# Weighing cached values eight pages at a time in every second tick of the first feed-forward stage

## The chip, the cores and the metric

The kernel runs on one core of a Trainium2 chip. The metric is the device time of one execution in microseconds (us), as the median of the runs. Fewer is better.

## The reference

One inference step of one layer, for a prompt of 1024 rows and for 8 samples of one row each, each with a past of 8192 positions in a paged cache (64 pages of 128 positions). The part that matters here, cut to its core:

```python
def half_ffn(x, g, w_gate, w_up, w_down):
    h = rmsnorm(x, g)
    return x + 0.5 * ((silu(h @ w_gate) * (h @ w_up)) @ w_down)
...
def sb_sample(q, k_new, v_new, bias, k_past, v_past):      # 8 samples, 8 heads of 64
    z = (q . [k_past, k_new]) * scale + bias
    w = sb_weights(z, q_pos, k_pos)       # exp(log_sigmoid(z) + sum of log_keep over later positions)
    o = w[..., :past] . v_past + w[..., past:] . v_new
...
x = half_ffn(x, ffn1 weights); then mixing (attention | state space), cross attention, half_ffn(ffn2 weights)
k_past = cache_k[l][page_table];  v_past = cache_v[l][page_table]
```

The product of the weights `w` with the cached values `v_past` is what the change moves. It adds up over all 64 pages of a sample.

## The kernel before, in words

The stages follow one another. The change is in `ffn1`, the first half feed-forward of the prompt (D_MODEL 1024, D_FF 2816), beside which the attention of the samples over the cache is done for six of the eight samples (scores for seven). The stage is a timetable of 132 ticks, written out by hand (`Timetable`), and every engine's program walks through the same ticks.

- **Feed-forward.** Twelve ticks make a group of 256 columns of D_FF. In ticks 0 to 7 of a group TensorE does one tile of 512 prompt rows of the gate or the up projection, in ticks 8 to 11 four tiles of the down projection. Each product of float32 quality is three matmuls (`three_passes`, L111 to L113) of split operands, so a tick has 24 such matmuls. VectorE and ScalarE split the weights (L84, L88), form the product of silu and up (L1763), and VectorE drains the down sums (`drain`, L1784). SP loads the weights.
- **Scores.** SP loads keys (`load_k`), 2 pages to a chunk in a ring of 4 chunks, and VectorE multiplies (L624) and reduces (L629) them: 32 chunks for a sample in 17 ticks (PERIOD).
- **Weights of a sample.** From its scores, ScalarE, VectorE and TensorE form the log weights: `page_sums` (L707) and `within_page` (L713) are single f32 matmuls that TensorE does at the end of a tick. L661 reads the result of L713.
- **Values.** GpSimd loads pages of values (`load_v`, L611) into a ring of VR = 8 pages, 256 KB each. TensorE weighs them in quads of four pages (`weigh`, L725): for each page c of four, a f32 matmul with 32 columns of weights and 512 columns of values, into rows 32c to 32c+31 of bank 6. In the trace each of these matmuls is two instructions, so a quad is eight. A sample has 16 quads. The last matmul of a quad adds one to `v_used`. Behind the last quad VectorE masks bank 6 (`own_heads`, L671), TensorE sums its columns (`columns`, L732) and ScalarE stores them.

The order on TensorE is `unit_tile` or four `down_tile` of the tick, and then `beside(t)`: first the quads of the tick, then `columns`, `page_sums` and `within_page`, each in its tick. Before a quad's matmul TensorE waits for the page (`v_in`). Before the load of page n GpSimd waits for the quad two quads earlier:

```python
def load_v(self, pool, n):
    if n >= self.VR:
        pool.wait_ge(self.v_used, n // 4 - self.VR // 4 + 1)
```

GpSimd's program loads the pages in their order and does nothing else in the stage after its constants. The quads of a tick are given by `Timetable.quads`: in the 17 ticks of a sample, ticks 0 to 13 have one quad each, tick 14 has two, ticks 15 and 16 none. Where a tick is named below it is this number within a sample's run.

Of the kernel before, what the change touches and what calls it, by code (L numbers as in the profile page):

```python
# [464 lines left out]
class Timetable:  # L465
# [32 lines left out]
    def quads(self, t):  # L498

        b, at = divmod(t - self.VALUES - (self.PERIOD - 1), self.PERIOD)  # L500
        if not (0 <= b < self.WEIGHED_HERE and at < self.V_TICKS):
            return range(0)
        return range(b * self.QUADS + at * self.QUADS // self.V_TICKS,
                     b * self.QUADS + (at + 1) * self.QUADS // self.V_TICKS)

    def weighed(self, t, after):

# [441 lines left out]
class Kernel:  # L949
# [1769 lines left out]
    def ssm(self):  # L2719
# [40 lines left out]

        groups_of = lambda i: slice(i // 2 * 8 + i % 2, i // 2 * 8 + 8, 2)
        quads, kinds = 0, {}
        for kind, n in (("gsum", 16), ("final", 1), ("y", 8), ("ysample", 8), ("turn", 9)):
            kinds[kind] = quads
# [758 lines left out]
```

## Time and profile before

| what | value |
|---|---|
| runs before | 2855.38 us median of 3 (2854.74 to 2855.69) |
| span of the profiled execution, first to last instruction | 2853.3 us |
| median of the runs less this span | 2.1 us |
| TensorE matmuls busy | 2621.2 us (92%) |
| VectorE busy | 2035.8 us (71%) |
| ScalarE busy | 849.0 us (30%) |
| GpSimd busy | 358.0 us (13%) |
| quads of the stage, first and last start | 358.7 to 1055.5 us |

The profile names the engines PE (TensorE matmuls), PEld (its weight loads), DVE (VectorE), ACT (ScalarE), POOL (GpSimd) and SP. A line number such as L725 is a line of the kernel. Matmuls are pipelined and overlap in the trace, so the distance from start to start says more than their durations; the four matmuls of a quad work in different columns of the array and start together.

### The profile page before, as it was taken

How to read it: one execution, taken by the hardware profiler on the slowest of the kernel's cores; microseconds unless marked ns; L12 is line 12 of the kernel's file. 1: busy time of each engine (PE TensorE's matmuls, PEld its weight loads, DVE VectorE, ACT ScalarE, POOL GpSimd, SP SyncE). 2: the span in 40 equal slices, each digit the busy share in tenths (PEclk: the TensorE clock that was granted, in tenths of full speed). 3: DMA queues.
4: the chain of work that ended last, by engine and by line, in shares of the span. 5: the costliest groups of instructions: out<-in, count | busy, mean ns of one | idle time of the engine just before them, and what ended most of it. 6: DMA issues, size and time to landing. Idle time of an engine off the chain costs nothing. (4 is left out here: it accounts for less than half of the span.)

```text
span 2853.3 us, 46035 instructions
## 1 busy us (share of the span) xinstructions
PE 2621.2 (92%) x15819; PEld 2119.1 (74%) x15819; DVE 2035.8 (71%) x2814; ACT 849.0 (30%) x1538; POOL 358.0 (13%) x588
## 2 busy tenths in 40 slices
PE   6779899999999999998858879998989999999998
PEld 4457666666666667875634679885879999999998
DVE  6549989899999956777764164528377777777767
ACT  4231212111122114018941352413233222222225
POOL 1010032322223220210022100024000000000000
PEclk8879999999999999999989999999989999999999
DMA  9876599989899953543158642126101111111121
GB/s 354 301 252 201 178 316 335 333 302 324 297 336 345 316 191 132 154 118 64 31 203 263 236 145 61 38 82 236 52 23 45 57 46 57 46 44 44 44 59 75
DMA packets 347045, 480.30 MB, mean 168 GB/s; under 512 B 35432, under 2 KB 228325, under 8 KB 345038
## 3 DMA queue, kind: packets, MB, share of 16 engines
q1 hardware_dynamic: 304006, 335.39, 35.6%
q0 software_dynamic: 42448, 142.33, 14.5%
q8 instruction: 95, 1.56, 0.2%
q14 instruction: 88, 0.72, 0.1%
q10 hardware_dynamic: 408, 0.31, 0.0%
HBM read 453.22 MB, written 22.62 MB: 167 GB/s over the span
## 5 line engine op out<-in xcount | busy, mean ns | idle before, releaser
L111 PE MATMUL banks<-ffn_ghi,whi 128*128 128x344 f32 (+1 forms) x880 | 318.1, 362 | 19.1 <-DVE xT L2258 10.4
L84 ACT ACTIVATE whi<-raw 128x1024 fp32r<-128x1024 f32 (+1 forms) x118 | 121.5, 1041 | 677.2 <-PE banks L113 583.2
L113 PE MATMUL banks<-ffn_ghi,wlo 128*128 128x344 f32 (+1 forms) x880 | 310.0, 352 | 0.0
L112 PE MATMUL banks<-ffn_glo,whi 128*128 128x344 f32 (+1 forms) x880 | 309.3, 351 | 0.0
L111 PE MATMUL banks<-a_hhi,whi 128*128 128x512 f32 x704 | 288.4, 410 | 6.9 <-DVE wlo L88 6.1
L624 DVE TENSOR_TENSOR ffn_kt<-ffn_kt,ffn_q 128x1024 f32<-128x1024 f32 x224 | 272.5, 1216 | 24.5 <-DMA ffn_kt<-in_cache_k_dram 24.4
L611 POOL DMA_DIRECT2D ffn_vt<-in_cache_v_dram x384 | 206.1, 537 | 656.5 <-issue 651.5
L113 PE MATMUL banks<-a_hhi,wlo 128*128 128x512 f32 x704 | 278.8, 396 | 0.0
L112 PE MATMUL banks<-a_hlo,whi 128*128 128x512 f32 x704 | 278.7, 396 | 0.0
L629 DVE TENSOR_REDUCE ffn_z<-ffn_kt 128x16 f32<-128x1024 f32 x224 | 272.5, 1217 | 5.7
L111 PEld LDWEIGHTS banks<-ffn_ghi,whi 128*128 128x128 f32 x880 | 166.4, 189 | 67.4 <-issue 22.6
L88 DVE TENSOR_TENSOR wlo<-raw,whi 128x1024 fp32r<-128x1024 f32 (+1 forms) x118 | 142.5, 1209 | 92.3 <-ACT whi L84 92.0
L111 PE MATMUL banks<-ffn_t_hi,whi 128*128 128x258 f32 x704 | 199.5, 283 | 1.7 <-DVE wlo L2165 1.0
L113 PE MATMUL banks<-ffn_t_hi,wlo 128*128 128x258 f32 x704 | 199.4, 283 | 0.0
L112 PE MATMUL banks<-ffn_t_lo,whi 128*128 128x258 f32 x704 | 199.3, 283 | 0.0
L111 PEld LDWEIGHTS banks<-a_hhi,whi 128*128 128x128 f32 x704 | 133.2, 189 | 82.9 <-issue 36.7
L113 PEld LDWEIGHTS banks<-ffn_ghi,wlo 128*128 128x128 f32 x880 | 166.5, 189 | 16.0
L112 PEld LDWEIGHTS banks<-ffn_glo,whi 128*128 128x128 f32 x880 | 166.8, 190 | 15.2 <-issue 1.2
L2069 ACT ACTIVATE whi<-raw 128x512 fp32r<-128x512 f32 x132 | 80.5, 624 | 314.3 <-PE banks L113 129.2
L111 PE MATMUL banks<-ffn_b_hi,whi 128*128 128x258 f32 x528 | 152.0, 288 | 7.3 <-DVE ffn_g L2202 7.3
L113 PEld LDWEIGHTS banks<-a_hhi,wlo 128*128 128x128 f32 x704 | 133.3, 189 | 31.4
L112 PEld LDWEIGHTS banks<-a_hlo,whi 128*128 128x128 f32 x704 | 133.4, 189 | 30.1 <-issue 1.9
(506 smaller groups left out, 5916.7 us busy)
## 6 DMA issues: line engine op xcount, KB each, us to landing
ffn_kt<-in_cache_k_dram SPq DMA_DIRECT2D x448, 256.0 KB, 4.3
ffn_vt<-in_cache_v_dram POOLq DMA_DIRECT2D x384, 256.0 KB, 5.0
raw<-in_w_ffn_gate_dram SPq DMA_DIRECT2D x44, 512.0 KB, 5.0
raw<-in_w_ffn_up_dram SPq DMA_DIRECT2D x44, 512.0 KB, 5.1
raw<-in_w_ffn_down_dram SPq DMA_DIRECT2D x44, 512.0 KB, 4.6
last_kt<-in_cache_k_dram POOLq DMA_DIRECT2D x64, 256.0 KB, 3.1
s_vt<-in_cache_v_dram POOLq DMA_DIRECT2D x64, 256.0 KB, 5.9
s_vt<-in_cache_v_dram SPq DMA_DIRECT2D x64, 256.0 KB, 7.7
```

Of the source, the lines that this page charges most:

```text
L84: act.activation(self.k.whi[c % W_RING][:, 0:self.width], self.slots[s][:, 0:self.width], ACT.Copy).then_inc(self.hi_done, 1)
L88: dve.tensor_tensor(self.k.wlo[c % W_RING][:, 0:self.width], self.slots[self.slot(n, c)][:, 0:self.width], self.k.whi[c % W_RING][:, 0:sel ...
L111: pe.matmul(out, whi, rhi, start=first, stop=False)
L112: pe.matmul(out, whi, rlo, start=False, stop=False)
L113: return pe.matmul(out, wlo, rhi, start=False, stop=last)
L611: pool.dma_start(self.vt[:, n % self.VR], self.values[:, ds(page, 1), :]).then_inc(self.v_in[n % self.VR], 16)
L624: v.tensor_tensor(keys, keys, q, ALU.mult).then_inc(self.k_times_q, 1)
L629: v.tensor_reduce(self.z[:, c * 16:(c + 1) * 16], self.kt[:, r].rearrange("p (h d) -> p h d", d=64), AX.X, ALU.add).then_inc(self.scored, 1)
L2069: act.activation(half_slot(self.whi, 7 * ph + o), SOURCE[o], ACT.Copy).then_inc(w_hi, 1)
```

## The change

`Timetable.quads` gives two quads to every even tick and none to the odd ones. The sixteen quads of a sample are then done in ticks 0, 2, ... 14, two in each.

```diff
@@ Timetable.quads
         b, at = divmod(t - self.VALUES - (self.PERIOD - 1), self.PERIOD)
         if not (0 <= b < self.WEIGHED_HERE and at < self.V_TICKS):
             return range(0)
-        return range(b * self.QUADS + at * self.QUADS // self.V_TICKS,
-                     b * self.QUADS + (at + 1) * self.QUADS // self.V_TICKS)
+        return range(b * self.QUADS + at, b * self.QUADS + at + 2) if at % 2 == 0 else range(0)
```

QUADS is 16 and V_TICKS is 15. Nothing else is edited. `quads_before`, from which GpSimd's loop takes how many pages to ask for in a tick, follows from it.

## Rows read from the trace of the kernel before

**Rows 1.** The page: span, and TensorE's busy time, share and instructions.

```profile
span 2853.3 us, 46035 instructions
...
PE 2621.2 (92%) x15819; PEld 2119.1 (74%) x15819; DVE 2035.8 (71%) x2814; ACT 849.0 (30%) x1538; POOL 358.0 (13%) x588
```

**Rows 2.** One stretch: us, busy and count by engine, clock, DMA share, GB/s.

```profile
478.00:598.00 120.00, 119.63 (x549) 80.39 (x548) 110.35 (x123) 22.61 (x28) 34.33 (x64) 1.00 0.91 319
```

**Rows 3.** Waits from 358 to 1069 us: total, times, longest.

```profile
PEld banks L725 <- DMA ffn_vt<-in_cache_v_dram: 17.1, 17, 2.7
...
PEld banks L111 <- DVE xT L1784: 5.0, 6, 1.2
```

**Rows 4.** TensorE's timeline, one ordinary tick: start, us, instructions, idle before.

```profile
478.23 0.39 PE L113 MATMUL banks<-a_hhi,wlo 128*128 128x512 f32 x1
478.55 1.06 PE L725 MATMUL banks<-ffn_vt,ffn_w 128*32 128x512 f32 x8
479.55 0.50 PE L111 MATMUL banks<-a_hhi,whi 128*128 128x512 f32 x1
479.88 0.39 PE L112 MATMUL banks<-a_hlo,whi 128*128 128x512 f32 x1
...
485.02 0.40 PE L113 MATMUL banks<-a_hhi,wlo 128*128 128x512 f32 x1
485.35 1.06 PE L725 MATMUL banks<-ffn_vt,ffn_w 128*32 128x512 f32 x8
```

**Rows 5.** TensorE's timeline, ticks 12 to 14 of the first sample.

```profile
440.65 1.07 PE L725 MATMUL banks<-ffn_vt,ffn_w 128*32 128x512 f32 x8
...
448.31 1.06 PE L725 MATMUL banks<-ffn_vt,ffn_w 128*32 128x512 f32 x8
...
455.08 2.05 PE L725 MATMUL banks<-ffn_vt,ffn_w 128*32 128x512 f32 x12
...
458.91 1.04 PE L725 MATMUL banks<-ffn_vt,ffn_w 128*32 128x512 f32 x2 [0.38 <-DMA ffn_vt<-in_cache_v_dram]
459.89 1.12 PE L713 MATMUL banks<-ffn_e,ffn_tri 128*128 128x512 f32 x2
```

**Rows 6.** The same, tick 14 of the last sample, from three starting points.

```profile
1052.63 1.92 PE L725 MATMUL banks<-ffn_vt,ffn_w 128*32 128x512 f32 x14
...
1053.09 1.46 PE L725 MATMUL banks<-ffn_vt,ffn_w 128*32 128x512 f32 x10
...
1053.52 1.03 PE L725 MATMUL banks<-ffn_vt,ffn_w 128*32 128x512 f32 x6
...
1055.98 0.70 PE L713 MATMUL banks<-ffn_e,ffn_tri 128*128 128x512 f32 x1
```

**Rows 7.** GpSimd's timeline: the issue of single pages.

```profile
450.61 0.55 POOL L611 DMA_DIRECT2D ffn_vt<-in_cache_v_dram  x1 [3.65 <-issue]
...
454.07 0.54 POOL L611 DMA_DIRECT2D ffn_vt<-in_cache_v_dram  x1 [0.61 <-issue]
...
480.86 0.54 POOL L611 DMA_DIRECT2D ffn_vt<-in_cache_v_dram  x1 [14.56 <-issue]
```

**Rows 8.** Landings of value pages: all; 457 to 466 us; issues at 360.98, 364.44, 1051.63.

```profile
DMA to landing us min/median/max: 2.8/5.0/7.2
...
DMA to landing us min/median/max: 4.2/4.6/5.8
...
DMA to landing us min/median/max: 3.8/3.8/3.8
...
DMA to landing us min/median/max: 4.4/4.4/4.4
...
DMA to landing us min/median/max: 3.3/3.3/3.3
```

**Rows 9.** GpSimd's timeline, a pause within four pages.

```profile
552.36 0.54 POOL L611 DMA_DIRECT2D ffn_vt<-in_cache_v_dram  x1 [3.20 <-issue]
```

**Rows 10.** VectorE's timeline, its wait behind tick 14.

```profile
461.05 0.69 DVE L661 TENSOR_TENSOR ffn_zb<-ffn_zb,banks 128x512 f32<-128x512 f32 x1 [1.43 <-PE banks L713]
```

## The prediction

> **What bounds the kernel now.** I read first the shares of the engines on the page: TensorE is busy for 2621 of 2853.3 us [rows 1]. The change touches one stage, so the table by stretch comes next. While cached values are weighed (358.7 to 1056 us), TensorE is busy in all but 0.4 us of a 120 us stretch at the full granted clock, VectorE in 110.35, and the transfers fill 91% of the 16 DMA engines [rows 2]. TensorE's stream of instructions sets the time. The waits of the stretch say what breaks it: 17.1 us of weight loads wait for a page of cached values, and 5.0 us for VectorE's drains of the sums [rows 3].
>
> Then TensorE's timeline. An ordinary tick of the planner takes 6.80 us (478.55 to 485.35) [rows 4]: 24 matmuls of the feed-forward, and between them one quad, four pages as eight instructions. The last tick of a sample holds two quads, 14 and 15, and there the timeline has holes: from 455.08 to 459.89 us it does 16 instructions of L725 [rows 5].
>
> **What the change does.** The same 96 quads run in the same order. Quads 1, 3, 5, ... 13 of each sample move one tick earlier, right behind their even neighbours: 7 in each of 6 samples, 42 in all. Tick 14 keeps its two. The pages are asked for in the same order by GpSimd, and each waits for the same count of used quads as before, so its program doesn't change; nor do the queue of SP, the chunks that VectorE scores, and the ticks of the softmax chain. No instruction is added or removed. Only the time at which the ring of eight pages empties and is wanted again changes.
>
> **First term, fewer changes between the two kinds of matmul.** Inside a tile the matmuls start 0.233 us apart (479.88 to 485.02 is 5.14 us over 22 steps [rows 4]). Around a lone quad the starts are 478.23, 478.55, 479.55, 479.88 [rows 4]: 1.65 us where two steps would be 0.47, so a quad by itself costs 1.18 us. A quad right behind another one is seen in tick 14 of the last sample: its groups of four start at 1052.63, 1053.09, 1053.52 and 1053.95 (the last by the same step), that is 0.43 us apart with two groups to a quad [rows 6]. A second quad costs 0.86 us. Each move saves 1.18 - 0.86 = 0.32 us; times 42 is 13.6 us (0.324 unrounded).
>
> **Second term, the holes of tick 14.** Two quads and the step to the next matmul need 0.86 + 1.00 = 1.86 us without a wait. Sample 0 takes 459.89 - 455.08 = 4.81 [rows 5], a hole of 2.95; the last one 1055.98 - 1052.63 = 3.35 [rows 6], a hole of 1.49. The six are 2.95, 3.43, 4.13, 3.02, 2.39 and 1.49, together 17.4 us, which agrees with the 17.1 in the waits [rows 3]. They arise because the pages of quad 15 are asked for behind quad 13, one tick before. In the new order they are asked for in tick 12, so these holes go. The two terms give 31.0 us.
>
> **Third term, what is late next.** GpSimd starts the first page 2.31 us after the quad that frees its place has started (478.55 to 480.86; also 448.31 to 450.61) and then one page each 1.155 us (450.61 to 454.07 is three steps) [rows 4, 5, 7]. Now it must fetch eight pages in a row for each pair. Call the start of a pair's first quad S. The eighth page is issued at S + 2.31 + 7 x 1.155 = S + 10.40. The next pair's second quad wants it at S + 2 x 6.775 - 0.32 + 0.86 = S + 14.09 (6.775 us is the mean of the ordinary ticks; the one in the rows has 6.80 [rows 4]). So a page has 3.69 us from issue to use. Before, outside tick 14, a fourth page had 2 x 6.775 - 2.31 - 3 x 1.155 = 7.8 us. Check of this arithmetic on tick 14 as it was: the fourth page behind quad 13 is issued at 454.07 and wanted at 455.08 + 0.86 = 455.94, 1.87 us later; its matmul starts at 458.91, 4.84 us after the issue [rows 5, 7]. That makes a hole of 2.97, against 2.95 by the step to the next matmul.
>
> What does a landing take? Over all 384 pages it is 2.8, 5.0, 7.2 us (least, median, most); the 84 fourth pages outside the first two quads of a sample have a mean of 5.11, the first of them 4.4 and the last 3.3 [rows 8]. With 0.05 us from landing to matmul, x = 5.16 - 3.69 = 1.47 us is missing at a pair. A hole gives time to the pages of the following pair, so a hole there is x less the one before: with equal landings they fall in ticks 2, 6, 10 and 14. The last has 0.88 us more, since a matmul of the softmax chain lies in tick 12 (448.31 - 440.65 = 7.66 us for that tick [rows 5]). That is 3 x 1.47 + 0.59 = 5.0 us per sample, 30.0 in six (24 x - 5.3). GpSimd also has pauses of its own: 3.20 us idle ahead of a page where 0.62 is usual [rows 9]; there are three of such length in the stage, two of them inside a sample's run, and some fifteen of 0.28 us more than usual. Ahead of eight pages on a tight budget they add about 2.6 us each and little for the small ones, some 6 us. Landings aren't equal, and a hole can't be negative, so uneven ones add more than even ones. I carried the recursion (hole = landing + 0.05 - 3.69 - the hole before, at least nothing) through all 42 pairs with the landings of the page issued nearest in time; shifted by 0 to 9 us it gives 32 to 41 us, and with draws from the fourth pages 44. I take 39.
>
> **Sum.** 39 - 13.6 - 17.4 = 8.0 us slower, against the profiled execution's 2853.3 us span; the median of the runs, 2855.38, is 2.1 us more, which is what lies around the span. 2855.4 + 8.0 = 2863 us.
>
> What else moves costs nothing while covered. VectorE has 8% idle in the stretch, some of it behind the hole of tick 14 itself (1.43 us at 461.05) [rows 2, 10]. Its work stays the same, TensorE's ticks become 5.6 and 7.6 us plus hole in turn. If the cover is gone in the short ticks, the 5.0 us of waits for drains [rows 3] may double: 0 to 5 us, which I take as nothing since the holes give it back.
>
> **A page's rule against this.** The rows show 5.0 us at the median from issue to landing and 2.8 at the least [rows 8]. The Trainium skill, page DMA: Bandwidth & Descriptors, section Anatomy of one DMA, gives a transfer issued by GpSimd as about 2.0 us plus its bytes over 436 GB/s. For 256 KB that is an estimate of 2.6 us, under the budget, so by it no pair would wait and the kernel would gain all that the first two terms give. The trace agrees only at its least landing.
>
> **Rivals.** (a) Pages land in time, the other side of the sign. With every landing under 3.6 us the change gives 2855.4 - 31.0 = 2824 us. It comes out faster than no change by 0.2% (5.7 us) when the holes are below 25.3 us. By 24 x - 5.3, with 6 for GpSimd's pauses and 3 for unevenness, this is x = 0.90, a last page that lands in 4.54 us on average and not 5.11. For it: the eight pages in a row that exist behind tick 14 landed no later than others (median 4.6 us for those from 457.38 on [rows 8]). Against it: there VectorE was between two samples and asked for few keys. Chance 0.15, typically 2847.
> (b) The terms cancel: landings of 4.5 to 5.0 for the last page, 2850 to 2861. Chance 0.33.
> (c) As forecast, holes of 37 to 50 us: 2861 to 2874. Chance 0.40.
> (d) The queue grows over eight pages. The 84 first pages, read as the fourth ones were, land in 4.55 us on average (the earliest in 3.8 [rows 8]), so 0.56 is added over three more pages; 0.2 us per page more up to the eighth would make 5.9, and the recursion gives about 60 us: 2855.4 + 60 - 31.0 = 2884. Against it: the transfers are full already at four pages, and GpSimd's pace of one per 1.155 us limits the queue. Chance 0.12, with anything between 2874 and there.
>
> So faster 0.15, same 0.33, slower 0.52, where 0.2% is about what a measurement here can tell from no change. The range leaves out the far half of (d) and most of (a): 2846 to 2880.
>
> **What would show it.** In the changed kernel: L725 in groups of 16 instructions; 1.86 us from such a group to the next tile where no wait falls; waits of weight loads for pages up from 17.1 to 35 to 45 us, spread over about 30 pairs as holes of 0.5 to 3 us; none of over 2 us in tick 14 as a rule; GpSimd's pages in runs of eight, 1.155 us apart. The prediction is wrong if landings of the eighth pages leave 5.1 us by 0.5 in either direction, if a second quad costs much else than 0.86 us, or if VectorE's drains hold up the short ticks.

## The result and the profile after

The change makes the kernel slower: a median of 2873.39 us against 2854.74 us before, a ratio of 1.0058 with a 95% interval of 1.0039 to 1.0076. That is 11 to 22 us, 16.6 us at the middle. The forecast was 2863 us, 8 us slower, with a range of 2846 to 2880 us: the sign is as forecast and the time lies in the range, but the change costs about twice what was forecast. The profiled execution has a span of 2868.9 us, 15.6 us over that of before [rows 1]. The page after, its span and shares:

```profile
span 2868.9 us, 46035 instructions
## 1 busy us (share of the span) xinstructions
PE 2635.4 (92%) x15819; PEld 2132.4 (74%) x15819; DVE 2036.5 (71%) x2814; ACT 849.7 (30%) x1538; POOL 358.1 (12%) x588
```

The number of instructions is the same, and so is VectorE's work. The stretch that corresponds to [rows 2] (columns: PE, PEld, DVE, ACT, POOL busy, then clock, DMA share, GB/s):

```profile
478.00:598.00 120.00, 118.86 (x533) 79.39 (x532) 107.50 (x119) 22.70 (x28) 34.34 (x64) 1.00 0.92 316
```

The clock is full and the transfers as busy as before, but TensorE does 533 matmuls in 120 us where it did 549. VectorE has more idle time than before, not less (busy 107.50 us, 110.35 before [rows 2]). The waits of the changed kernel between 340 and 1100 us name the place (total, times, longest):

```profile
PEld banks L724 <- DMA ffn_vt<-in_cache_v_dram: 44.3, 54, 2.1
...
DVE ffn_kt L623 <- DMA ffn_kt<-in_cache_k_dram: 29.5, 10, 5.9
...
PEld banks L111 <- DVE xT L1783: 4.6, 3, 3.5
```

Weight loads waited 17.1 us for pages of values before [rows 3] and wait 44.3 us now, in 54 places. The lines of the changed kernel are one less than those of before from the edit on. The waits for VectorE's drains haven't grown.

A pair is the two quads of an even tick, 16 instructions of L724; a hole is time that a pair takes beyond 1.86 us because it waits. TensorE's timeline shows two pairs, one without a hole and one with:

```profile
386.04 1.92 PE L724 MATMUL banks<-ffn_vt,ffn_w 128*32 128x512 f32 x16
387.89 0.50 PE L111 MATMUL banks<-a_hhi,whi 128*128 128x512 f32 x1
...
399.24 3.83 PE L724 MATMUL banks<-ffn_vt,ffn_w 128*32 128x512 f32 x16
403.00 0.51 PE L111 MATMUL banks<-a_hhi,whi 128*128 128x512 f32 x1
```

The pair at 386.04 is followed by the next tile after 1.85 us. Two ticks take 13.20 us (386.04 to 399.24) where they took 13.55. Then the pair at 399.24 needs 3.76 us, a hole of 1.90. GpSimd's timeline between the two, and the landing (the time from issue until the page is there) of the page issued last:

```profile
388.35 0.54 POOL L610 DMA_DIRECT2D ffn_vt<-in_cache_v_dram  x1 [6.72 <-PE banks L724]
...
395.27 0.54 POOL L610 DMA_DIRECT2D ffn_vt<-in_cache_v_dram  x1 [0.62 <-issue]
396.43 0.54 POOL L610 DMA_DIRECT2D ffn_vt<-in_cache_v_dram  x1 [0.62 <-issue]
```

```profile
DMA to landing us min/median/max: 5.6/5.6/5.6
```

The first page goes 2.31 us behind the pair's start, the eighth 10.39 us behind it. It lands at 402.03. The second quad of the next pair wants it at 399.24 + 0.86 = 400.10, so the hole is 1.93 us by this count and 1.90 by the timeline.

Over the whole run I compare the stage by one length: from the start of the first quad to the first matmul after the last one. It leaves out what differs ahead of the stage from one execution to the next: the first quad starts anywhere from 346 to 365 us in the traces of this study, so single spans aren't compared for a few microseconds. Each kernel's stage is read from one trace. Before it is 1055.98 - 358.67 = 697.3 us, after 1069.57 - 357.20 = 712.4. The holes are what a group of L725 or L724 takes over 1.86 us (1.00 for a lone quad). Before they are 17.4 us in the six ticks 14 and 0.4 in one tick 12. After they are 47.5 us in 27 of the 48 pairs.

### The profile page after: what moved, and what is told of

Its sections match the earlier page's. It is cut to its first block and busy times, and to the rows that moved or that the text cites. A ratio compares the mean times of both kernels' runs of the same rounds, so it can differ in the third digit from the quotient of the medians.

```text
span 2868.9 us, 46035 instructions
## 1 busy us (share of the span) xinstructions
PE 2635.4 (92%) x15819; PEld 2132.4 (74%) x15819; DVE 2036.5 (71%) x2814; ACT 849.7 (30%) x1538; POOL 358.1 (12%) x588
```

## The experiments

Each ran beside the kernel before on the same chip. In the table, "stage" is the length just defined, "holes" the sum over the groups, and "other" is the stage less its holes less 665.9 us (697.3 - 17.4 - 0.4 - 42 x 0.324: the stage with every pair together and no wait, by the forecast's own first term; for one quad per tick the single quads are added back). For one quad in each of 16 ticks the last, extra tick of 5.9 us is taken off. The kernels with fixed pages, with half the keys and with less VectorE each leave out a part of the computation. The ratio counts the whole kernel, and outside the stage the profiled executions differ by up to 20 us ahead of it and 10 us behind it, so the stage is the better measure of what an edit did there.

| kernel | ratio to before, 95% | stage | holes | other |
|---|---|---|---|---|
| before | 1 | 697.3 | 17.8 | 0 |
| changed | 1.0058 (1.0039 to 1.0076) | 712.4 | 47.5 | -1.0 |
| changed, ring of 10 | 0.9945 (0.9926 to 0.9964) | 681.7 | 6.4 | 9.4 |
| before, ring of 10 | 0.9954 (0.9931 to 0.9977) | 684.4 | 2.9 | 1.9 |
| changed, fixed pages | 0.9918 (0.9889 to 0.9947) | 672.3 | 2.8 | 3.7 |
| one quad in each of 16 ticks | 0.9945 (0.9923 to 0.9967) | 684.4 | 2.5 | 0.5 |
| changed, half the keys | 0.9983 (0.9962 to 1.0003) | 699.8 | 34.7 | -0.8 |
| changed, ring of 10, less VectorE | 0.9884 (0.9846 to 0.9923) | 674.8 | 5.5 | 3.4 |
| changed, ring of 10, query later | 0.9936 (0.9912 to 0.9959) | 683.5 | 8.3 | 9.3 |
| changed, numbers read ahead | 0.9939 (0.9915 to 0.9962) | 678.8 | 8.2 | 4.7 |
| changed, ahead and ring of 10 | 0.9919 (0.9898 to 0.9940) | 671.6 | 0.0 | 5.7 |

**A ring of 10 pages, changed kernel.**

```diff
-    VR = 8
+    VR = 10
...
-            pool.wait_ge(self.v_used, n // 4 - self.VR // 4 + 1)
+            pool.wait_ge(self.v_used, (n - self.VR) // 4 + 1)
```

> The changed kernel with a ring of 10 value pages and not 8, so that two pages of each pair may be asked for a tick earlier and the last page of a pair is issued 2 x 1.155 = 2.31 us sooner. Theory A (a pair waits for its last page, which GpSimd issues eighth in a row at 1.155 us each): the time from issue to use grows from 3.69 to 6.0 us, nearly all of the 47 us of holes go, a few us stay behind GpSimd's own pauses and landings over 6 us: 2855 - 31 + 3 = 2827 us, 1.0% faster than before. Rival B (values land late because the transfers are full, whenever they are asked for): the landings move with the issues and 30 us or more of holes stay, about 2855 us or above. Rival C (uneven ticks, VectorE holding up the short ones): 2865 us or above, with TensorE's idle time at drains and not at pages.

The holes fall from 47.5 to 6.4 us, as theory A has it, and rivals B and C fall with them: the pages land in time once they are issued two places earlier, though the last page of a pair, now the sixth that GpSimd issues in a row, still lands in 5.4 us. But the gain is 0.55% and not 1.0%. TensorE waits elsewhere. Its timeline, and VectorE's at the same place:

```profile
801.55 0.39 PE L113 MATMUL banks<-a_hhi,wlo 128*128 128x512 f32 x1
806.38 0.95 PE L731 MATMUL banks<-ones,ffn_own 128*128 128x1 f32 x5 [4.44 <-DVE ffn_own L670]
```

```profile
802.98 1.22 DVE L88 TENSOR_TENSOR wlo<-raw,whi 128x1024 fp32r<-128x1024 f32 x1
804.12 0.68 DVE L660 TENSOR_TENSOR ffn_zb<-ffn_zb,banks 128x512 f32<-128x512 f32 x1
804.83 0.69 DVE L663 TENSOR_TENSOR ffn_zb<-ffn_zb,ffn_own 128x512 f32<-128x512 f32 x1
805.63 0.69 DVE L670 TENSOR_TENSOR ffn_own<-banks,ffn_mask 128x512 f32<-128x512 f32 x1
```

VectorE runs without a gap and comes to the mask of the finished sample (L670) only at 805.63, so that the columns (L731) start 4.4 us late. At this sample's end, the fourth, 7.9 us are lost altogether: from its last pair to the next sample's first are 28.4 us, where others take 20.5. The wait is only a part of that. Right behind it TensorE's granted clock is at the lower of its two levels (1.2 GHz, 0.50 in the row) for 6.8 us; the columns are as in [rows 2]:

```profile
806.70:813.50 6.80, 6.80 (x20) 5.57 (x20) 6.70 (x8) 0.18 (x1) 0.00 (x0) 0.50 0.79 264
```

There the feed-forward's matmuls start 0.43 us apart (808.40, 808.83, 809.26) and not 0.233, which costs an estimated 3.1 us (6.8 x (1 - 0.233 / 0.43)). The kernels before and changed have the full clock in the whole stage.

**The same ring in the kernel before.** The two edits above, without the change.

> The kernel before with a ring of 10 pages, one quad per tick as it was. Theory A: the holes of tick 14 (2.95, 3.43, 4.13, 3.02, 2.39, 1.49 us) each shrink by 2.31 us, to 4.4 us together: 13 us less than before, 2842 us (0.46% faster). The distance from here to the changed kernel with a ring of 10 is then the first term alone, 42 x 0.32 = 13.6 us, and 1 or 2 us of holes. Rival B: the holes of tick 14 stay, 2855 us. Rival D (a second quad in a row saves nothing in sum): this kernel and the changed one with the same ring come out equal.

It came out as theory A says: the stage is 12.9 us shorter (13 expected), the holes are 2.9 us (4.4 expected). By the first term the changed kernel with the same ring should be 13.6 us shorter again; its stage is 2.7 us shorter, and the two ratios can't be told apart. Rival D named this outcome, but not the reason: holes and other delays (15.8 us against 4.8) take 11.0 of it, and a pair of ticks does cost 13.20 us and not 13.55.

**Pages of fixed number.**

```diff
-        page = pool.value_load(self.pages[0:1, n:n + 1], min_val=0, max_val=639)
-        pool.dma_start(self.vt[:, n % self.VR], self.values[:, ds(page, 1), :]).then_inc(self.v_in[n % self.VR], 16)
+        pool.dma_start(self.vt[:, n % self.VR], self.values[:, n:n + 1, :]).then_inc(self.v_in[n % self.VR], 16)
```

> The changed kernel in which GpSimd reads no page number: value page n of the pool is loaded for entry n, so the page table of the values is left out, all else as it was. It tests GpSimd's pace. Theory A: if the pace falls from 1.155 us a page by d, the last of eight is issued 7 d sooner; with d of 0.3 us or more the holes fall from 47 to under 10 us and the time to 2825 to 2835 us. If the pace stays, the time stays at some 2872 us. Rival B (full transfers): pages issued sooner land later by as much, holes stay over 30 us, 2857 us or more whatever the pace.

GpSimd's timeline in this run:

```profile
432.93 4.23 POOL L609 DMA_DIRECT2D ffn_vt<-in_cache_v_dram  x8 [9.03 <-PE banks L723]
```

Eight pages take 4.23 us, 0.53 each. The median landing rises from 5.2 us to 6.1 in the stretch from 358 to 1030 us, so rival B has a part in it: pages asked for faster do land later, the eighth of a run in 7.57 us on average where it took 5.42. But these 2.15 us stand against an issue 5.3 us sooner (5.09 us behind the pair's start and not 10.41 at the median: 4.4 by the pace and 0.9 because the first page goes sooner too), and the holes are gone but for 2.8 us.

**One quad in each of 16 ticks.** The kernel before with `V_TICKS = 16`.

> The kernel before with V_TICKS 16: one quad in each of ticks 0 to 15 of a sample, no double tick, and the masking, columns and store one tick later. Theory A: the holes of tick 14 (17.4 us) go and six quads that stood right behind another stand alone, 6 x 0.32 = 1.9 us: 15.5 us less than before, 2840 us (0.54% faster), with no wait for a page in ticks. Rival E (the later masking and store hold up the next sample's first quad): 1 to 3 us for each of 5 samples, 2845 to 2855 us.

The stage is 12.9 us shorter than before, against 15.5 expected; 2.5 us of holes stay where none was expected. The ratio of 0.9945 is 15.7 us. By the stage rival E is out, since "other" is only 0.5 us. So what the ring of 10 gives the old order (12.9 us too) comes without a larger ring, from not doubling the last tick.

**Half the keys.**

```diff
-            sp.dma_start(self.kt[:, n % self.KR, j * 512:(j + 1) * 512], self.keys[:, ds(page, 1), :]).then_inc(self.k_in[n % self.KR], 16)
+            wide = 512 if n < self.KR or j == 0 else 16
+            sp.dma_start(self.kt[:, n % self.KR, j * 512:j * 512 + wide], self.keys[:, ds(page, 1), 0:wide]).then_inc(self.k_in[n % self.KR], 16)
```

> The changed kernel with half of the key traffic: of each chunk's two key pages the second is loaded only in its first 16 columns (after the first four chunks), so the scores are left wrong by that part; VectorE's work and GpSimd's program stay. It asks how much of a landing is owed to the keys beside it. Theory A1 (the eighth page's 5.4 us landing is mostly contention with the keys): it lands near the least value seen, 3 to 4 us, under the 3.69 us from issue to use, and the holes fall from 47 us to under 12; time 2830 to 2840 us. Rival A2 (the landing is what eight value pages in a row cost by themselves): it stays over 5 us, holes stay at 35 us or more, time 2860 us or more.

Neither. The same stretch as above, and the waits between 350 and 1050 us:

```profile
478.00:598.00 120.00, 118.50 (x542) 80.85 (x542) 107.89 (x122) 19.96 (x26) 33.73 (x63) 1.00 0.76 246
```

```profile
PEld banks L725 <- DMA ffn_vt<-in_cache_v_dram: 32.1, 46, 1.9
```

With the DMA share down from 0.92 to 0.76 and the rate from 316 to 246 GB/s, the eighth page lands in 4.76 us on average (5.42 in the changed kernel), and the holes fall to 34.7. That is 12.8 us for 0.66 us of landing, and the forecast's 24 us of holes per microsecond would say 15.8. So this half of the keys makes 0.7 us of a landing and 12.8 of the 47.5 us of holes; both theories had the size wrong. What a landing would be with no keys beside it no run shows. The ratio of 0.9983 isn't in conflict with a stage 2.5 us longer than before: key loads are left out ahead of the stage too, and it counts the whole kernel.

**Less work for VectorE, ring of 10.** In `score_heads`, for every fourth chunk:

```diff
+        if c % 4 == 3:
+            v.memset(self.z[:, c * 16:(c + 1) * 16], 0.0).then_inc(self.scored, 1)
+            return
```

> The changed kernel with a ring of 10 pages and less work for VectorE: in every fourth chunk the sum over a head's 64 columns is left out (a small memset in its place), 1.2 us of VectorE less for each of 56 chunks. The ring of 10 alone gave a stage 15.6 us shorter than before where 31 was possible: 6.4 us of holes and 9.4 us of other delay. Theory F (the other 9.4 us are VectorE's, which comes late to the masking and the drains once TensorE's sample takes 115 us): they go, the stage shrinks to 673 us, some 9 us less than with the ring alone, 2830 us. Rival G (they come from TensorE's order or the transfers): the time stays within 3 us of the ring of 10.

"Other" falls from 9.4 to 3.4 us, the holes stay (5.5), the ratio goes from 0.9945 to 0.9884. The stage is 6.9 us shorter than with the ring alone; the ratios differ by 17 us, of which the rest lies outside the stage and isn't explained here (four executions of this kernel). Theory F holds for two thirds of the 9.4 us; 3.4 stay, nearly all at the fourth sample's end, where the step from the last pair to the next sample's first takes 24.0 us and 20.5 at the others. There TensorE waits 1.6 us for VectorE's mask (4.4 before this edit), and then the lower clock of 3.4 us, half as long as before the edit, costs an estimated 1.6.

**The query later, ring of 10.** In `load_k` the query's load moves from a sample's first chunk to behind its third.

```diff
-        if c == 0:
+        if c == (self.KR - 1 if b else 0):
             if b:
-                sp.wait_ge(self.k_times_q, n)
+                sp.wait_ge(self.k_times_q, b * 32)
```

> The changed kernel with a ring of 10 pages, and the query of the next sample loaded behind that sample's first three chunks of keys and not ahead of them, so that its wait for VectorE's last multiply no longer holds up these keys. Whole computation. Theory F: VectorE waits 27 us for keys in the stage; with 1 to 3 us less at each of 6 sample starts the other 9.4 us of delay halve: 4 to 6 us less than the ring alone, 2836 us. Rival G: no difference from the ring of 10 alone.

No gain in the stage: "other" is 9.3 us as with the ring alone, and the intervals of the two ratios overlap. The waits of VectorE say why.

```profile
DVE ffn_kt L623 <- DMA ffn_q<-qs_scratch: 25.0, 5, 5.6
...
DVE ffn_kt L623 <- DMA ffn_kt<-in_cache_k_dram: 3.4, 3, 1.9
```

The 27 us that stood under the keys now stand under the query. The query waits for VectorE's last multiply of the sample before, since it has a single buffer, and it lands too late by itself; to load the keys sooner doesn't help as long as that is so.

**Page numbers read ahead.** Whole computation. GpSimd reads eight numbers before the waits of a pair:

```diff
                     for n in range(begun, until if t >= plan.PERIOD + 2 else 0):
-                        d.load_v(pool, n)
+                        if n % 8 == 0:
+                            pages = [pool.value_load(d.pages[0:1, m:m + 1], min_val=0, max_val=639) for m in range(n, n + 8)]
+                        d.load_v(pool, n, pages[n % 8])
```

> The changed kernel, whole computation, in which GpSimd reads the eight page numbers of a pair into registers before it waits for the first quad, and then issues the eight loads without a read between them. Ring of 8 as it was. Theory A (holes come from GpSimd's 1.155 us a page, of which some 0.6 us is the read of the page number): the pace falls to about 0.53 us as with fixed pages, the eighth page is issued some 4 us sooner, the holes fall from 47 us to about 3 and the stage from 712 to about 673 us, with landings about 1 us longer; time as with fixed pages, a ratio of 0.992 to before, 2835 us. Rival H (the fixed pages were fast because they lie side by side in memory and not because the number wasn't read): the pace or the landings stay, holes over 20 us, ratio 0.998 or above.

```profile
441.21 4.69 POOL L609 DMA_DIRECT2D ffn_vt<-in_cache_v_dram  x8 [9.68 <-PE banks L723]
```

The pace falls to 0.59 us a page, and the first page goes 1.75 us behind the pair's start (439.46) where it was 2.31. The eighth page is issued 5.90 us behind the pair's start and lands in 7.17 us on average. The stage is 678.8 us with 8.2 us of holes, where 673 and 3 were expected; the largest hole, 2.4 us, is again at the pair whose run of loads has a pause of 2.6 us. Rival H is out: the pace came with the number's read, not with where the pages lie.

**Both, read ahead and a ring of 10.**

> As the run with page numbers read ahead, and a ring of 10 pages. Theory A with F: neither pace nor ring leaves holes; what stays is 4 to 9 us of delay by VectorE, so this is within 3 us of the better of the two parts, a ratio of 0.991 to 0.994. Were the two to add, it would be 0.987.

No hole is left, and TensorE doesn't wait for a page anywhere in the stage. The stage is 671.6 us, 40.8 less than the changed kernel. It is 7.2 us shorter than the better of the two parts, where at most 3 were expected; the ratio lies in the range expected. "Other" is 5.7 us, with these waits from 350 to 1050 us:

```profile
PEld banks L730 <- DVE ffn_own L669: 5.0, 3, 2.8
PE banks L730 <- DVE ffn_own L669: 3.7, 2, 2.3
```

Behind the wait at the fourth sample's end the clock is at its lower level for 3.4 us here too, an estimated 1.6 us of the 5.7. This beats both kernels, 0.9919 (0.9898 to 0.9940) of before. The intervals of all the versions from 0.9918 to 0.9945 overlap, so which of them is best isn't settled by the times.

## Why the prediction was right, and where its sizes were off

- **Where the time goes.** Right: the lateness of the last page of a pair. The ring of 10, the fixed pages and the numbers read ahead each take away 39 to 45 of 47.5 us of holes by another way of having the page sooner, without a change in TensorE's order.
- **First term, fewer changes of matmul kind.** Right, a little small. A pair of ticks without a hole takes 13.204 us, 0.346 under 2 x 6.775, and 42 times that is 14.5 us, against 13.6 forecast; the -1.0 of "other" in the changed kernel is about this difference.
- **Second term, the holes of tick 14.** Right. Of 17.4 us, 2.5 stay, in two samples. The forecast had counted what stays in the third term.
- **Third term, the new holes.** The mechanism was right and the size too small: 47.5 us against 39. The issue of the eighth page (10.39 against 10.40 us behind the start) and its budget (3.67 us with the pair of 13.20, against 3.69) were met. Its landing wasn't: 5.42 us on average over 42, where the forecast took over the 5.11 of fourth pages. By the forecast's own 24 us of holes per microsecond, 0.31 us more is 7.4 of the 8.5 us that were missing. The landing rises along the run, as rival (d) said, but by less: first 3.95, third 4.80, fourth 4.97, fifth 5.11, seventh 5.36, eighth 5.42 us. GpSimd's pauses did what was written: two of 3.2 us idle fell within a run inside a sample (552 to 556 and 758 to 761 us), and the pairs that wait for these pages have the two largest holes, 4.20 and 3.2 us. The third fell in a run between two samples and made none.
- **Sum.** 47.5 - 14.5 - 17.4 - 0.4 = 15.2 us, against 15.1 measured in the stage and 16.6 by the ratio; the forecast was 39 - 13.6 - 17.4 = 8.0. So the sign came from the mechanism that was forecast, but it was a close call: the forecast gave "slower" a chance of 0.52, and its own rival with landings of 4.5 to 5.0 us for the last page had the terms cancel.
- **VectorE's cover.** Right for this change, where the holes give VectorE the time. It is gone as soon as they go: with a ring of 10 TensorE waits for VectorE's mask, and with the lower clock behind that wait "other" is 9.4 us. The forecast's rival (a), 2824 us if all pages land in time, left both out. The run without holes shows 5.7 us of them.
- **The page's rule.** By the Trainium skill (DMA: Bandwidth & Descriptors, Anatomy of one DMA) a page would land in an estimated 2.6 us. The least in the changed kernel is 2.7, the median 5.1. With the DMA share at 0.76 it is 4.2. The kernel before has one short stretch with freer transfers, 1048 to 1055 us with a share of 0.53, and its last pages, issued from 1048 to 1052 us, land in 2.9 to 3.3 us: near the rule and still above it. So the measured landings decide here, and the rule alone would have given the wrong sign.

What stays open: the 3 to 6 us of "other" that are left once VectorE has less to do or no hole exists. With fixed pages, with less VectorE and with both edits the timeline lays 3 to 4 us of them to the wait for the mask at the end of the fourth sample (1.6 to 2.3 us) and to the lower clock behind it (3.4 us long, an estimated 1.6 us), but no run took either away. Why the clock falls there isn't shown: in the changed kernel the longest hole, 4.20 us, is followed by the full clock.

## What to carry to other kernels

Before work is put together in larger batches, count when the last input of a batch is issued and when it is wanted: a ring of exactly one batch is empty when the batch ends, and then the loads of the whole batch must be issued one after another within one period. Here the average rate was unchanged and only the budget of the last page fell from 7.8 to 3.7 us, under its landing of 5.4. When the engine that bounds is made faster, look at what the next one's idle time was worth, and look at the granted clock in the same place; here VectorE's lateness and the lower clock behind it took most of the 9.4 us by which the larger ring, holes aside, fell short of the 31 forecast.

## What the hardware showed that was not expected

- Reading a page number into a register costs GpSimd 0.6 us each time between two loads (1.155 us a page with it, 0.53 with a fixed address). With the numbers of eight loads read before the wait, the reads fall into time in which GpSimd would wait anyway, and the loads follow each other in 0.59 us.
- The landing of a value page is longer the further back it stands in a run at 1.155 us each, 3.95 us for the first and 5.42 for the eighth. With the ring of 10, where a run begins two pages later, it rises with the place in the run all the same, from 4.25 us for the first to 5.59 for the eighth. At 0.53 us each it is 4.12 for the first and 7.57 for the eighth.
- GpSimd's stream of loads pauses at the same pages in both orders: 0.28 us more at about every 21st, and 2.6 us more at pages 113, 219 and 325. With fixed pages the small ones are gone and the large ones are at the same three pages (2.2 to 2.5 us); with the ring of 10 they are at 113, 217 and 321. What GpSimd does there no row shows.
- TensorE's granted clock can fall inside a stage that otherwise has all of it: in six of the kernels, all with two quads to a tick and at most 8.3 us of holes, it is at the lower level for 3.4 or 6.8 us, each time behind a wait of TensorE for VectorE (0.8 to 4.4 us).
